# Outputs and solve of two slabs issued alternately behind the fourth couple

## What is computed

```python
def step(s, xt):
    wt, kt, vt, kkt, at = xt[:5]
    sa = jnp.einsum('bhvk,bhk->bhv', s, -kkt)
    s = (s * wt[:, :, None, :] + sa[..., None] * (kkt * at)[:, :, None, :]
         + vt[..., None] * kt[:, :, None, :])
    if r is None:
        return s, None
    return s, jnp.einsum('bhvk,bhk->bhv', s, xt[5])
```

## Time and profile before

| | |
|---|---|
| median of 3 runs | 4121.16 us (4111.47 to 4129.18) |
| profiled execution, its time | 4116.76 us |
| profiled execution, its span | 4114.9 us |
| mean granted TensorE clock | 0.962 of 2.4 GHz |
| TensorE matmul busy | 3772.4 us (92%) |
| VectorE busy | 2290.6 us (56%) |
| ScalarE busy | 1947.2 us (47%) |
| GpSimd busy | 613.5 us (15%) |

### The profile page before, as it was taken

One profiled execution on the slowest core, in us unless ns is written; L12 is line 12 of the kernel. 1 busy time (PEld: TensorE's weight loads), 2 busy tenths in 40 slices (PEclk: granted clock), 3 DMA queues, 4 the chain that ended last, 5 costly groups with the idle time before them and its releaser, 6 DMA issues. The chain is left out here.

```text
span 4114.9 us, 93756 instructions
## 1 busy us (share of the span) xinstructions
PE 3772.4 (92%) x39634; PEld 3168.5 (77%) x39634; DVE 2290.6 (56%) x3788; ACT 1947.2 (47%) x3029; POOL 613.5 (15%) x601
## 2 busy tenths in 40 slices
PE   7999999999979899989898978997599999999993
PEld 6778878888868788888887767786488888888883
DVE  5533524434337777777776975455554545454445
ACT  5533434434336666666665443243144444444443
POOL 1000000000012122212210333200011111111111
PEclk9999999999989999999998989998699999999997
DMA  7566565555542222222323466654366666666667
GB/s 277 189 180 190 179 194 152 159 155 157 151 119 76 80 76 66 80 80 62 105 64 90 117 222 215 197 181 160 148 210 215 211 213 213 212 217 209 219 209 296
DMA packets 334966, 673.42 MB, mean 164 GB/s; under 512 B 32828, under 2 KB 213156, under 8 KB 316936
## 3 DMA queue, kind: packets, MB, share of 16 engines
q1 hardware_dynamic: 307592, 580.68, 43.3%
q0 software_dynamic: 27008, 87.46, 7.4%
HBM read 524.89 MB, written 143.15 MB: 162 GB/s over the span
## 5 line engine op out<-in xcount | busy, mean ns | idle before, releaser
L112 PE MATMUL fro__acc<-fro__hT_hi,fro__wh 128*128 128x512 f32 (+1 forms) x1608 | 626.0, 389 | 11.8 <-DVE fro__hT_lo L2671 8.9
L113 PE MATMUL fro__acc<-fro__hT_hi,fro__wl 128*128 128x512 f32 (+1 forms) x1608 | 614.3, 382 | 0.0
L114 PE MATMUL fro__acc<-fro__hT_lo,fro__wh 128*128 128x512 f32 (+1 forms) x1608 | 614.1, 382 | 0.0
L2677 DVE TENSOR_TENSOR fro__wl<-prj__w,fro__wh 128x1024 fp32r<-128x1024 f32 x201 | 246.2, 1225 | 640.6 <-ACT fro__wh L2460 640.6
L2088 DVE TENSOR_TENSOR fin__wl<-fin__raw,fin__wh 128x4096 fp32r<-128x4096 f32 x96 | 424.6, 4423 | 318.4 <-ACT fin__wh L2032 318.4
L2032 ACT ACTIVATE fin__wh<-fin__raw 128x4096 fp32r<-128x4096 f32 x96 | 348.4, 3629 | 190.4 <-PE exp__acc L114 190.3
L112 PE MATMUL exp__acc<-fin__wh,exp__xh 128*128 128x512 f32 x1024 | 400.9, 391 | 0.7 <-DVE exp__xl L2093 0.7
L113 PE MATMUL exp__acc<-fin__wh,exp__xl 128*128 128x512 f32 x1024 | 399.3, 390 | 0.0
L114 PE MATMUL exp__acc<-fin__wl,exp__xh 128*128 128x512 f32 x1024 | 399.2, 390 | 0.0
L112 PEld LDWEIGHTS fro__acc<-fro__hT_hi,fro__wh 128*128 128x128 f32 x1608 | 304.7, 189 | 77.9 <-issue 22.2
L113 PEld LDWEIGHTS fro__acc<-fro__hT_hi,fro__wl 128*128 128x128 f32 x1608 | 304.8, 190 | 59.2 <-issue 3.6
(11 more groups left out here) (460 smaller groups left out, 8121.9 us busy)
## 6 DMA issues: line engine op xcount, KB each, us to landing
fin__raw<-in_w_x SPq DMA_DIRECT2D x96, 2048.0 KB
prj__w<-in_w_z SPq DMA_DIRECT2D x201, 512.0 KB, 4.2
s_zT<-fro__pool SPq DMA_DIRECT2D x128, 256.0 KB, 4.7
fro__wm<-in_w_mod POOLq DMA_DIRECT2D x16, 1024.0 KB, 5.6
mix__gate<-s_zT SPq DMA_DIRECT2D x64, 256.0 KB, 4.3
prj__xin<-in_tokens SPq DMA_DIRECT2D x18, 512.0 KB, 5.4
rwc__kS<-s_kS SPq DMA_DIRECT2D x36, 256.0 KB, 3.1
rwc__kkn<-s_kkn SPq DMA_DIRECT2D x36, 256.0 KB, 3.3
```

The source lines that it names most:

```text
L112: pe.matmul(out, sh, mh, start=first, stop=False)
L113: pe.matmul(out, sl, mh, start=False, stop=False)
L114: return pe.matmul(out, sh, ml, start=False, stop=last)
L2677: ve.tensor_tensor(wl[s % 3][:, :, :], w[s % 3][:, :, :], wh[s % 3][:, :, :], ALU.subtract).then_inc(split_lo, 1)
```

## The change

A new function, `outputs_and_solve(j, i)`, makes both waits of the outputs and of the solve and then issues their matmuls in turns: one of the outputs of slab j's second chunk, one of the solve of slab i's first chunk, eight times. The two sets take their operands from the same half of the partitions and write to different halves (and to different PSUM banks). It stands where `solve(p, 0)` stood, behind `couple(3, h)`; the outputs no longer stand ahead of `couple(3, h)`. It is used where both slabs exist, h = 2 to 36. At h = 1 there is only a solve, at h = 37 only outputs, and these stay. ScalarE's, VectorE's and GpSimd's programs and the DMAs are not changed.

```diff
+            def outputs_and_solve(j, i):
+
+                v, z, o = j % B, side(turn_of(j, 1)), side(1 - turn_of(j, 1))
+                x = side(turn_of(i, 0))
+                pe.wait_ge(S["uc1"], at("uc1", j))
+                pe.wait_ge(S["rhc0"], at("rhc0", i))
+                pe.wait_ge(S["gd"], at("gd", i))
+                for n in range(WH):
+                    c = slice(WD * n, WD * n + WD)
+                    y = mm(PB[1][o, c], BK[v][z, n, 1, :], U[1][z, c], start=False, stop=True, skip_group_check=True)
+                    m = mm(PB[0][x, c], Gr[i % 2][x, n // GH, n % GH, :], R[0][x, c], start=True, stop=True)
+                y.then_inc(S["ym1"], 1)
+                m.then_inc(S["uum0"], 1)
...
-                if exists(h - 2):
+                if exists(h - 2) and not exists(p):
                     outputs(h - 2, 1)
                 if inverting:
                     couple(3, h)
-                if exists(p):
+                if exists(h - 2) and exists(p):
+                    outputs_and_solve(h - 2, p)
+                elif exists(p):
                     solve(p, 0)
                 if inverting:
                     double(3, h)
```

## The result

The changed kernel takes 4168.3 us (median of 4 runs, 4158.0 to 4182.4) against 4116.3 for the kernel before beside it: ratio 1.0124, 95% interval 1.0100 to 1.0148. It is some 50 us slower. I had named 4134 us, with a range up to 4156, and held "the same" for the likeliest. A second set of runs of the same kernel gave 1.0178 (1.0139 to 1.0217).

What follows compares the result with a forecast made beforehand. This part of the half step was taken as bound by ScalarE's yo, U, Tb, then TensorE from couple to pairs; 14.2 + 1.2 = 15.4 us of delay gave 4132.2 or 4136.6, named 4134 us, own range 4121 to 4147, wider 4108 to 4156.

Steps and rivals of the forecast that it cites:

- the same: Whole kernel: time within about 0.5% (20.6 us) of the kernel before, chance 0.63.
- The pair: Alternating outputs and solve behind the fourth couple: 32 instructions in 1.15 us, relieving TensorE of about 0.9 us.
- The relief falls into a gap: Ahead of the fourth couple: it waits for Tb as before, so removing the outputs there leaves TensorE idle.
- ScalarE's delay: ScalarE's yo waits for the pair, 0.52 us late in even half steps, 0.37 in odd; U, Tb and fifth couple follow.
- the sum: Whole kernel: 14.2 us of delay in half steps 2 to 33 plus 1.2 in 35 and 36, 15.4 us slower.
- slower, clock: Rival, couple to solve: TensorE's clock falls to 1.2 GHz; every third half step 15 us more, all 4176; chance 0.10.
- All 0.9 us fall into a gap: TensorE ahead of the fourth couple: the 0.9 us saved per half step gains no time; nothing is relieved behind it.

Runs made afterwards that it cites:

- e2: The changed kernel with 4 extra matmuls, results unused, between the fourth double and the fifth couple; ratio 1.0039 to the kernel before.
- e5: The kernel before with the second chunk's outputs moved behind the fourth couple, not alternated: all outputs, then the solve; ratio 1.0037.
- e10: The changed kernel with the alternating pair put ahead of the fourth couple instead of behind it; ratio 1.0050 to the kernel before.
- e8: The changed kernel run again, unaltered; ratio 1.0178 to the kernel before.
- e3: The kernel before with the second chunk's outputs, in their old place, cut to the last of their 8 matmuls; ratio 1.0020.
- e1: The changed kernel with 8 extra matmuls, results unused, in the outputs' old place ahead of the fourth couple; ratio 1.0068.

## Why the prediction was wrong

**The pair: right.** 32 instructions in 1.15 us were forecast; in half step 18 they run from 1737.80 to 1738.95. One row half and two banks do not hinder the overlap.

**The relief falls into a gap: right.** The fourth couple starts at 1.17 us in even half steps as before, and the fourth double at 2.94 to 2.97.

**ScalarE's delay: right in its kind, a little large.** yo is 0.45 us late in the median of the even half steps and 0.31 in the odd ones, against 0.52 and 0.37 forecast. I had put 0.03 us for the pair's longer issue and 0.04 for the lag on top of the solve's old end. But yo waits only for the last of the outputs, which ends 0.04 us ahead of the last of the solve, and the pair as a whole ends no later than the solve did alone. e2 and e5, which have the delay without the falls behind it, measure 16 and 15 us, and the sum had 15.4. That agreement is closer than it deserves, and partly luck. The intervals go from 9 to 23 us; e5's fifth couple is 0.53 and 0.38 us late and not 0.46 and 0.31 as in the changed kernel, and its late falls are longer than those before the change; and the untouched half steps of the changed kernel are longer by 0.24 us in the mean, 8 us in all. In the median the delay is still there at the first double of the next slab, 20 us on: 0.44 us in even half steps and 0.28 in odd ones, which would be 12 us. The order's own price is thus some 8 to 12 us in these half steps, where the sum had 14.2.

**The rival "slower, clock": the step that failed.** The sum of 15.4 us has no term for the clock; it takes all that TensorE does behind the delay at its old length. What stands in that place is 35 us, by e2 against the changed kernel (57 us by the second set of runs). The clock was left to a rival, which had the sign and the engine, a chance of 0.10, 15 us if every third half step were hit, and 4176 us if all were; the measured 4168 lies between the two, but not for the reasons given. Three things were wrong in it. Its place: I looked for the fall in the couple and the solve, and it comes 4 to 6 us behind the third double, in state and decays, after both gaps. Its size: I priced the doubling of 1.3 us of work, but the fall covers state, decays, the fifth double and pairs, which VectorE waits for, and costs about 2.6 us. Its frequency: 20 of 32 half steps are touched in one profile and 13 in the other, which was its fastest execution; one in three would be 11, so this was the smallest of the three faults. The row I had for it, a clock of 0.98 in a window, showed that the clock was not safely at its upper level in this stage; I read it as a small number instead of asking how near to falling the stage was. The sum of idle time around the change would have asked it. Between third double and fifth couple of half step 18 there was one wait of 0.42 us; by my own forecast there would be one of nearly 0.5 us ahead of the fourth couple and one of 0.9 us ahead of the fifth.

**"All 0.9 us fall into a gap": right, but taken as harmless.** Saved time was a cost. e5 against the changed kernel shows it, and e10 against the kernel before points the same way.

The Trainium skill ("TensorE: Matmul & The Clock Gate", section "HAM oscillation — how this bites in real kernels") ties the fall of the clock to pauses between bursts of matmuls; in its example they are waits for DMA of about 3 to 5 us. The traces agree in kind only. In half step 18 the clock falls behind waits of 0.48 and 0.86 us with thin work around them, pauses much shorter than the example's, and it took both the delay and the thin work for most of the falls.

**Open.** What exactly the clock goes by is not settled. The idle time of TensorE between third double and fifth couple, summed over all waits, goes with the falls only roughly. The table has its median in even and odd half steps, from the matmul records, and in how many of the 32 half steps with decays a fall begins 3 to 8 us behind the third double.

| kernel | idle, us, even and odd | falls |
|---|---|---|
| before | 0.45, 0.46 | 1 |
| changed | 1.38, 1.10 | 16 |
| e8, changed again | 1.38, 1.10 | 12 |
| e10, pair ahead of the couple | 1.08, 0.93 | 6 |
| e5, behind the couple in sequence | 1.07, 0.73 | 0 |
| e3, before, outputs thinned | 0.89, 0.76 | 5 |
| e2, filler behind the double, 4 | 0.89, 0.74 | 0 |

e5 has as much idle time as e10 in the even half steps and no falls, and e2 has what e3 has and none. Within the changed kernel the 16 half steps with such a fall and the 16 without it have the same idle time, 1.30 and 1.32 us in the mean, so the idle time of this stretch does not decide by itself. Nor does the number of matmuls decide: e1 has more than the kernel before, and falls. I did not vary the two waits one by one at constant work.

## What to carry to other kernels

Matmul time that is saved beside a gap is not simply worth nothing: here it lowered TensorE's clock for what comes behind the gap. Before a change that thins TensorE's work, add up its waits over the stretch before and after, and look whether the granted clock is already below 1 there. When an output is moved later on one engine, read who stands behind its copy on the next engine; the copy of an output that nobody waits for belongs behind the copies that the chain waits for.

## What the runs showed of the hardware

Four matmuls whose result is thrown away (8 instructions, 0.65 us) in each half step made a kernel faster by 35 us, with the decays back from 365 to 293 ns each.

In e5, the solve's first instruction starts at 1731.43 while the outputs' last ones, issued before it, start at 1731.49 to 1731.60: matmuls to different parts of the array do not keep to the order in which they are issued.

```profile
1731.43 0.27 PE L841 MATMUL rwc__PB<-rwc__R,rwc__Gr 64*64 64x64 f32 x1
1731.49 0.22 PE L863 MATMUL rwc__PB<-rwc__U,rwc__BK 64*64 64x64 f32 x1
```
